# Layer 1 of a two-layer mixer: two more heads' queries beside the last recurrence, and two output jobs inside memory attention

## The reference

```python
def memory_attention(mq, mk, mv):                      # 4 heads of 128, 256 memory rows
    sc = jnp.einsum('bshd,bmhd->bhsm', mq, mk) * (MEM_HEAD_DIM ** -0.5)
    p = jax.nn.softmax(sc, axis=-1)
    return jnp.einsum('bhsm,bmhd->bshd', p, mv).reshape(B, S, MEM_W)

def lru_mixer(h, w_in, conv_w, conv_b, wa, ba, wx, bx, lam):
    xb, gate, mq = jnp.split(h @ w_in, [LRU_WIDTH, 2 * LRU_WIDTH], axis=-1)
    xc = centred_depthwise_conv(xb, conv_w, conv_b)
    y = rg_lru(xc, ..., False) + rg_lru(xc, ..., True)  # a scan forward and one backward
    return y * jax.nn.gelu(gate), mq.reshape(B, S, MEM_HEADS, MEM_HEAD_DIM)

# in first_block, for l = 1
h = rms_norm(x, mix_norm[l])
mixed, mq = lru_mixer(h, ...)
mo = memory_attention(mq, mk, mv)
x = x + jnp.concatenate([mixed, mo], axis=-1) @ w_out[l]
```

## Time and profile before

| | |
|---|---|
| median of 3 runs | 3652.66 us (3648.69 to 3657.25) |
| the profiled execution | 3656.96 us, span 3655.2 us |
| instructions | 44517 |
| mean granted PE clock over the span | 0.987 |
| PE busy over the span | 96% |
| last gate matmuls of the recurrence to the start of output job 2 | 1611.20 to 1740.99 us |
| PE busy within 1611.2 to 1741.0 | 101.44 us of 129.80 |

### The profile page before, as it was taken

The page is one execution under the profiler, slowest core; times in us unless marked ns, Lnnn a source line. Parts: engine busy times, 40 slices in busy tenths (PEclk is TensorE's granted clock), DMA queues, the critical chain, the costliest instruction groups (busy, mean ns, idle before and its releaser), DMA issues. The chain is left out here.

```text
span 3655.2 us, 44517 instructions
## 1 busy us (share of the span) xinstructions
PE 3515.4 (96%) x16494; PEld 2883.7 (79%) x16494; DVE 1723.2 (47%) x1938; ACT 984.6 (27%) x1592; POOL 1060.7 (29%) x588
## 2 busy tenths in 40 slices
PE   7989989999999999979999999999999999999999
PEld 6878878888888886757888888888688888767877
DVE  6346662533434356874254343436535434443444
ACT  3346750201010115753020101012433233202011
POOL 0111033333333330013333333333245354322350
PEclk9999999999999999989999999999999999999999
DMA  5110012111111121110211111111211111111241
GB/s 181 37 34 19 20 38 86 58 52 46 52 46 46 52 80 70 43 55 18 86 58 51 47 46 52 46 50 51 79 58 51 46 61 43 55 43 52 92 133 75
DMA packets 58439, 210.87 MB, mean 58 GB/s; under 512 B 6672, under 2 KB 11280, under 8 KB 56672
## 3 DMA queue, kind: packets, MB, share of 16 engines
q1 hardware_dynamic: 47504, 159.67, 13.4%
q10 hardware_dynamic: 10832, 49.84, 3.7%
HBM read 186.15 MB, written 22.02 MB: 57 GB/s over the span
## 5 line engine op out<-in xcount | busy, mean ns | idle before, releaser
L536 PE MATMUL G<-Hhi,whi 128*128 128x512 f32 x2528 | 1010.5, 400 | 17.0 <-issue 5.1
L536 PE MATMUL G<-Hhi,wlo 128*128 128x512 f32 x2528 | 987.3, 391 | 0.0
L536 PE MATMUL G<-Hlo,whi 128*128 128x512 f32 x2528 | 987.2, 391 | 0.0
L424 POOL CAST whi<-wraw 128x1024 fp32r<-128x1024 f32 (+1 forms) x255 | 266.2, 1044 | 2311.6 <-PE G L536 1096.7
L426 POOL TENSOR_TENSOR wlo<-wraw,whi 128x1024 fp32r<-128x1024 f32 (+1 forms) x255 | 625.3, 2452 | 20.4
L536 PEld LDWEIGHTS G<-Hhi,whi 128*128 128x128 f32 x2528 | 476.6, 189 | 127.4 <-issue 20.2
L536 PEld LDWEIGHTS G<-Hlo,whi 128*128 128x128 f32 x2528 | 476.7, 189 | 101.2 <-issue 5.7
L536 PEld LDWEIGHTS G<-Hhi,wlo 128*128 128x128 f32 x2528 | 476.1, 188 | 100.4
L536 PE MATMUL G<-Uhi,whi 128*128 128x512 f32 x1024 | 398.5, 389 | 0.0
L536 PE MATMUL G<-Uhi,wlo 128*128 128x512 f32 x1024 | 398.5, 389 | 0.0
L536 PE MATMUL G<-Ulo,whi 128*128 128x512 f32 x1024 | 398.5, 389 | 0.0
(11 more groups left out here) (341 smaller groups left out, 4759.5 us busy)
## 6 DMA issues: line engine op xcount, KB each, us to landing
wraw<-wjobs SPq DMA_DIRECT2D x292, 512.0 KB, 3.3
scratch<-X ACTq DMA_DIRECT2D x2, 4096.0 KB, 14.0
gate_tiles<-gate_st ACTq DMA_DIRECT2D x16, 512.0 KB, 2.9
T<-gate_tiles ACTq DMA_DIRECT2D x16, 512.0 KB, 3.6
X<-xT ACTq DMA_DIRECT2D x1, 4096.0 KB, 16.4
X<-xT ACTq DMA_DIRECT2D x4, 1024.0 KB, 4.9
X<-scratch ACTq DMA_DIRECT2D x4, 1024.0 KB, 4.9
X<-scratch SPq DMA_DIRECT2D x4, 1024.0 KB, 11.5
```

What stands on the lines that cost most here:

```text
L424: pool.tensor_copy(whi[:, par, 0:kt], wraw[:, par, 0:kt]).then_inc(w_hi, 1)
L536: mm = pe.matmul(G[:, par, cols], w[:, par, k, :], x[:, k, cols], start=(k == 0 and j == 0), stop=(k == kt - 1 and j == 2))
```

## The change

- The query jobs of heads 1 and 2 are made directly behind the last gate matmuls, in `lru`. Head 3's is made beside units 0 to 9.
- DVE's `memory_queries` takes a whole head at a time (1024 columns): head 0 before `behind(7, 1)`, head 1 in its middle, head 2 behind it, head 3 at unit 10. The four heads have places of their own (`MQ`), two of them where the recurrence had its inputs.
- The attention uses only `G[:, 0]` (`mem_bank`). Head 3's job and output jobs 0 and 1 use `G[:, 1]`, one behind the other: units 0 to 9, 12 to 21 and 24 to 31 with 1 or 2 parts a unit (`fill`), none in units 10, 11, 22 and 23. PE's unit 0 needs head 0, the scores of unit 2 need head 2's queries.
- Output job 0 takes the feature tiles in the order 0, 6, 1, 7, 2, 3, 4, 5. ACT casts tiles 6 and 7 at units 10 and 12, DVE subtracts at units 12 and 14. DVE adds job 0 to X at unit 22 (`add_output`), job 1 behind the attention.

```diff
@@ job_part: psum half and order of feature tiles may be given
-                k, c = q // halves, q % halves
+                i, c = q // halves, q % halves
+                k = order[i]
@@ mem_attention of PE
+                    plan = ([(0, q) for q in range(16)], [(1, q) for q in range(16)], [(2, q) for q in range(16)])
+                    fill = {}
+                    for first, counts, parts in zip((0, 12, 24), ((2, 1, 2, 1, 2, 2, 1, 2, 1, 2),) * 2 + ((2,) * 8,), plan):
+                        for v, count in enumerate(counts):
+                            fill[first + v] = [parts.pop(0) for _ in range(count)]
...
+                    if l:
+                        if v == 0:
+                            pe.wait_ge(evac[e], 3 + BASE[name][e])
+                        if v == 2:
+                            pe.wait_ge(evac[e], 3 + BASE[name][e] + 2)
+                        if v == 3 * NBLK:
+                            pe.wait_ge(evac[e], 3 + BASE[name][e] + 3)
+                        queries = MQ[h]
...
+                    if l:
+                        for m, q in fill.get(h * NBLK + u, ()):
+                            n = START[name] + 3 + m
+                            if q == 0:
+                                pe.wait_ge(evac[e], BASE[name][e] + (4 if m == 0 else 5 + m))
+                            job_part(q, n, n % 2, Hhi, Hlo, mixed_ready(1) if m else None, psum=1,
+                                     order=(0, 6, 1, 7, 2, 3, 4, 5) if m == 1 else range(KT))
@@ lru of PE
+                for h in range(1, 3):
+                    psum_waits("mq1", h, h % 2)
+                    job(START["mq1"] + h, h % 2, Hhi, Hlo, None)
@@ mem_attention of DVE
-                    if l and h + 1 < MEM_HEADS and u in (4, 7):
-                        memory_queries(h + 1, u // 7)
-                    elif l and h + 1 == MEM_HEADS and u in (4, 6):
-                        mixed_low(1, EARLY + u // 6)
+                    if l and v == 10:
+                        memory_queries(3)
+                    elif l and v in (12, 14):
+                        mixed_low(1, EARLY + v // 14)
+                    elif l and v == 22:
+                        add_output(1, 0, 1)
@@ lru of DVE
-                behind(7, 1, first_queries)
+                memory_queries(0)
+                behind(7, 1, lambda: memory_queries(1))
+                memory_queries(2)
```

More of the change, by code:

```diff
@@ L166, in build @@
         eps_col = stat[:, 30:31]
+        MQ = [T[:, 0, :], sb("MQ1", [P, S], F32, U_AT + 4 * KB)[:], sb("MQ2", [P, S], F32, U_AT + 9 * KB)[:], T[:, 1, :]]
         Q = [sb("Q0", [P, 2, S], F32, R_AT + 8 * KB), T]
@@ L356, in scored, with mem_bank, mixed_ready @@
             return G[:, par, 0:width] if u % 3 == 2 else AUX[:, u % 3, 0:width]
+        def mem_bank(l, h):
+            return 0 if l else h % 2
+        def mixed_ready(l):
+            return lambda k: (early_lo, EARLY * l + k + 1) if k < EARLY else (split_lo[l], k - EARLY + 1)
         block = ctx.enter_context(nc.Block())
@@ L523, in psum_waits, with job_part @@
                     pe.wait_ge(evac[o], (2 + BASE[name][o] if other is None else other + 2) - (par == 0))
-            def job_part(q, n, par, hi, lo, ready, kt=KT, width=S):
+            def job_part(q, n, par, hi, lo, ready, kt=KT, width=S, psum=None, order=range(KT)):
                 half = min(width, 512)
                 halves = width // half
-                k, c = q // halves, q % halves
+                i, c = q // halves, q % halves
+                k = order[i]
                 if q == 0:
@@ L535, in job_part @@
                 for j, (w, x) in enumerate(((whi, hi), (whi, lo), (wlo, hi))):
-                    mm = pe.matmul(G[:, par, cols], w[:, par, k, :], x[:, k, cols],
-                                   start=(k == 0 and j == 0), stop=(k == kt - 1 and j == 2))
+                    mm = pe.matmul(G[:, par if psum is None else psum, cols], w[:, par, k, :], x[:, k, cols],
+                                   start=(i == 0 and j == 0), stop=(i == kt - 1 and j == 2))
                 if q == kt * halves - 1:
@@ L626, in scores @@
                         pe.wait_ge(s["pr"], done + v - 2)
[L627 to L631, removed]
+                    if l:
[6 more added lines that the diff above has]
+                        queries = MQ[h]
+                    else:
+                        if b == 0:
+                            pe.wait_ge(mq_raw, h + 1)
+                        if b == 4:
+                            pe.wait_ge(evac[e], 3 + BASE[name][e] + h)
+                        queries = T[:, h % 2, :]
+                    pe.matmul(scored(mem_bank(l, h), v, 2 * P), queries[:, b * P:(b + 1) * P], MK[:, h, :], start=True, stop=True)\
                       .then_inc(s["sc"], 1)
@@ L654, in turn_result @@
                         pe.wait_ge(s["oc"], done + v)
-                    pe.transpose(G[:, v // NBLK % 2, 512:512 + P], o[:, v % 2, :], ident).then_inc(s["ot"], 1)
+                    pe.transpose(G[:, mem_bank(l, v // NBLK), 512:512 + P], o[:, v % 2, :], ident).then_inc(s["ot"], 1)
                 def beside(h, u):
-                    if h + 1 < MEM_HEADS:
+                    if l:
[5 more added lines that the diff above has]
+                                     order=(0, 6, 1, 7, 2, 3, 4, 5) if m == 1 else range(KT))
+                    elif h + 1 < MEM_HEADS:
                         for q in {1: (0, 1), 2: (2, 3), 3: (4, 5), 4: (6, 7), 5: (8, 9, 10), 6: (11, 12, 13), 7: (14, 15)}.get(u, ()):
@@ L664, in beside @@
                             pe.wait_ge(s["oc"], done + (MEM_HEADS - 1) * NBLK)
[L665 to L671, removed]
+                        for q in range(3 * u - 6, min(3 * u - 3, 16)):
+                            next_part(q, START[name] + MEM_HEADS, 0, shift, eng=e)
                 scores(0)
@@ L824, in project_out @@
             def project_out(l):
[L825 to L831, removed]
+                name, ready = f"wo_mixed{l}", mixed_ready(l)
                 pe.wait_ge(*((attns["am"]["oc"], 2 * MEM_HEADS * NBLK) if l else (attns["aw"]["oc"], KT * NBLK)))
[L833 to L837, removed]
+                if l == 0:
+                    psum_waits(name, 1, 1)
+                    for q in range(12):
+                        job_part(q, START[name] + 1, 1, Hhi, Hlo, ready)
+                    for j in range(2):
+                        for q in range(12, 16):
+                            job_part(q, START[name] + j, j, Hhi, Hlo, ready)
                 with pe.Fori(1, 4) as i:
@@ L1264, in exp @@
                     t = v % 4
-                    act.activation(pr[:, v % 2, 0:2 * P], scored(v // NBLK % 2, v, 2 * P), ACT.Exp, bias=stat[:, 4 + t:5 + t],
+                    act.activation(pr[:, v % 2, 0:2 * P], scored(mem_bank(l, v // NBLK), v, 2 * P), ACT.Exp, bias=stat[:, 4 + t:5 + t],
                                    scale=MEM_SCALE, accum_out=stat[:, 8 + t:9 + t]).then_inc(s["pr"], 1)
@@ L1276, in result @@
                     wait_apart(act, s["ot"], done + v + 1)
-                    act.copy(mo[:, h, b * P:(b + 1) * P], G[:, h % 2, 512:512 + P]).then_inc(s["oc"], 1)
+                    act.copy(mo[:, h, b * P:(b + 1) * P], G[:, mem_bank(l, h), 512:512 + P]).then_inc(s["oc"], 1)
                 if l == 0:
@@ L1291, in mem_attention @@
                         query_raw(h + 1, u // 7)
-                    elif l and h + 1 == MEM_HEADS and u in (3, 5):
+                    elif l and v in (10, 12):
                         act.wait_ge(job_done, START["wo_mixed1"])
-                        mixed_high(1, EARLY + u // 5)
+                        mixed_high(1, EARLY + v // 12)
                 result(U - 2)
@@ L1759, in start, with memory_queries @@
                 norm("nmix0", lambda k: vcol("mix_norm", k))
[L1761 to L1769, removed]
+            def memory_queries(h):
+                dve.wait_ge(job_done, START["mq1"] + h + 1)
+                dve.tensor_tensor(MQ[h], G[:, h % 2, :], rstd_1[:], ALU.mult).then_inc(evac["dve"], 1)
             def mem_attention(l):
@@ L1779, in peak @@
                     wait_apart(dve, s["sc"], done + v + 1)
-                    chain.link(dve.reduce_max(mx, scored(v // NBLK % 2, v, 2 * P), AX_X))
+                    chain.link(dve.reduce_max(mx, scored(mem_bank(l, v // NBLK), v, 2 * P), AX_X))
                     dve.tensor_scalar(negm, mx, -MEM_SCALE, None, ALU.mult).then_inc(s["mx"], 1)
@@ L1993, in mixed_low, with add_output @@
                 dve.tensor_tensor(Hlo[:, k, :], mixed[:, k, :], Hhi[:, k, :], ALU.subtract).then_inc(split_lo[l], 1)
+            def add_output(l, m, par):
+                dve.wait_ge(x_back[m // 2], l * 16 + 16)
+                dve.wait_ge(job_done, START[f"wo_mixed{l}"] + m + 1)
+                dve.tensor_tensor(X[:, m, :], G[:, par, :], X[:, m, :], ALU.add).then_inc(evac["dve"], 1)
             def project_out(l):
@@ L1997, in project_out @@
```

(11 more changed lines are left out.)

## The result

The changed kernel takes 3633.34 us (median of 7 runs, 3626.17 to 3638.30), against 3656.55 for the kernel before in the same comparison (7 runs): a ratio of 0.994 (95% interval 0.993 to 0.9949), 19 to 26 us less. The forecast was 22.2 us.

The account below looks back on a forecast made before the run. PE, busy 96% of the span, bounds the kernel, so only its idle time can be gained. Summed terms put job 2 at 1718.8 against 1740.99, 22.2 us less: 3652.66 - 22.2 = 3630.5 us, range 3622 to 3641.

Parts of the forecast that it names:

- The term of 4.1 us for the later first maximum: Attention's start: first row maximum 4.1 us later than before, first turn at 1640.2; bounds 1.25 to 6.7 us.
- The first split: POOL's split of head 3's weights meets the recurrence's last block; DVE's first L2115 (later L2151) ends 2.2 us late.
- The second: POOL's split of output job 0's weights: its cast holds the last product of DVE's recurrence for 0.8 us.
- The order forecast: End of DVE's recurrence: the sum, at 1633.0, comes before POOL's cast of output job 0's weights, at about 1633.3.
- The clock at the start: Behind PE's wait for head 2's queries (1633.8 to 1637.5), PE runs 3.6 us at the lower clock, 1.2 GHz.
- The units: Attention units on PE: 1.29 us without parts, 1.95 with one part, 2.60 with two.
- The rival in which DVE and ACT pace them: Attention units: PE no longer covers DVE and ACT, 0.5 us lost on each of 16 units; 3638.5 us, chance 0.26.
- The rival of one half of G: Attention in one half of G ties PE, DVE and ACT together; at 1 us a unit 3662.5 us, chance 0.04.
- Tiles 6 and 7: Output job 0: PE waits 2.3 us at unit 13 and 0.5 at unit 16; the clock costs another 1.7.
- The row at 1718.40: Kernel before: clock fell after a PE wait of 1.97 us; used for the 1.7 us clock cost at tile 6.
- POOL's tiles and job 1's weights: Output jobs: POOL's tiles 1 to 5 ready before their units, job 1's weights ready before unit 24.
- The tail: Attention's end: the time from the end of unit 31 to 1726.12 in the kernel before stays 2.8 us.

Follow-up runs that it names:

- the third experiment: Changed kernel with output job 0's tiles in the order 0, 1, 6, 2, 7, 3, 4, 5; 104.01 us from gates' end to job 2, ratio 0.9929.
- first: Changed kernel with output job 0's weights split on POOL only after DVE finished the recurrence; 104.59 us from gates' end to job 2, ratio 0.9922.
- second: Changed kernel with output job 0's and head 3's weights split only after DVE finished the recurrence; 106.32 us from gates' end to job 2, ratio 0.9926.
- the fourth experiment: Changed kernel with 8 of head 3's 16 parts put in PE's wait for head 2's queries; 103.24 us from gates' end to job 2, ratio 0.9923.
- the seventh: Changed kernel with output job 1 moved out of units 24 to 31, behind the attention; job 2 starts 113.3 us behind the gates' start, ratio 0.9936.
- head 1 alone: Kernel before with only head 1's query job moved behind the last gate matmuls; 128.79 us from gates' start to job 2, ratio 0.9985.
- fifth: Changed kernel with late split of output job 0's weights, its tiles reordered, and 8 head 3 parts in PE's wait; 3621.21 us, ratio 0.9903.
- sixth experiment: Changed kernel with 24 useless matmuls filling PE's wait for head 2's queries; 110.63 us from gates' start to job 2, ratio 0.9934.

## Why the prediction was right, point by point

- **The place and the size.** PE's idle time at the start of the attention is what the change uses: 22.2 us forecast, 23.4 in the stretch (135.19 to 111.75), 21.7 from the gates' end, about 22 by the ratio; the median of 3633.34 us lies within the 3626 to 3635 that the forecast gave itself. Job 2 was to start 107.6 us behind the gates' end; it starts at 108.05. Two errors of opposite sign hide in that, 2.2 us too little at the start and 1.7 too much at tile 6. The mechanism was right; that the sum came out so close is luck.
- **The start was mis-sized.** The term of 4.1 us for the later first maximum measured 6.3 (1630.22 - 1601.72 = 28.5 us behind the gates' end, before 1633.42 - 1611.20 = 22.2). The first split was right to a tenth (L2151 3.32 us). The second was to hold DVE for 0.8 us and held it for 2.7, which is 1.9 of the 2.2 us. The step that failed is the order of two instants, put at 1633.0 for the sum and 1633.3 for POOL's cast, taken from an execution whose gates ran at half clock; in the profile after they ran at full clock, PE's two jobs ended 0.6 us earlier against DVE's chain, and the cast came first. PE's wait was 5.99 us for it, where 3 to 5 had been forecast. The order forecast is seen in the third experiment, with 26.1 us against 26.3 forecast. The mechanism is shown by the first two, in which the long instructions are gone with the meeting. The rule of the Trainium skill ("SBUF — State Buffer", "Who interferes with whom"), that whichever is first holds the other for the whole instruction, agrees with both starts: the same split costs DVE's chain 0.7 or 2.7 us.
- **The clock at the start** fell as forecast (0.50 for 3.6 us), and costs 1.1 us of the path by the filled wait.
- **The units** were right: 1.90 us with one part (1.95 taken), 2.59 with two, 1.29 without, also in a row. The rival in which DVE and ACT pace them is refuted by the fourth experiment, and by the seventh but for waits of 0.67 and 0.18 us. The rival of one half of G is refuted with it.
- **Tiles 6 and 7.** The waits were 1.55 and 1.19 us, forecast 2.3 and 0.5. The clock did not fall behind the first (1.00), where the forecast took 1.7 us by a wait of 1.97; behind one of 2.38 in the fourth experiment it did. This 1.7 is what paid for the start. The row at 1718.40 was thin ground: with head 1 alone a wait of 1.97 us too, behind three shorter ones much as there (0.36, 0.54, 0.58), left the clock at full:

```profile
1711.00:1713.00 2.00, 1.97 (x11) 1.67 (x12) 0.00 (x0) 0.07 (x1) 1.92 (x2) 1.00 0.00 0
```

- **POOL's tiles and job 1's weights** were in time, as forecast.
- **The tail** is 3.1 us instead of 2.8. The trace names DVE's addition of job 1 for the last 0.84 us before job 2, though the code has job 2 wait for job 0's alone. PE waits there for ACT's last copy too; with job 1 in this place, in the seventh experiment, PE stood for 0.45 us. What the other 0.4 us are stays open.

## What to carry to other kernels

Where PE stands in front of a chain of another engine, a finished operand and a free half of PSUM are enough to put jobs there, and each is worth its length less what it makes the chain slip, as long as PE is the bound elsewhere (head 1 alone: 11.0 us of job, 3.1 of slip, 6.4 gained in all); ask next which later work their end triggers, for here it was two splits on POOL that fell into the very chain that PE waited for. A wait that has been shortened but not closed can still cost the clock behind it (5.99 and 2.38 us did here, 0.56 and 1.55 did not), so fill it first. Compare kernels over a stretch between two instructions that both have, and say in which state of the clock it began: here 5.40 or 3.70 us for the same eight matmuls, at times as much as an edit is worth.

## What the runs showed of the hardware

- Two-operand instructions of DVE in SBUF and POOL's, in the same time, wait for each other as wholes: L2151 3.32 us for 1.2, L2161 3.25 for 1.2, POOL's difference 3.20 for 2.4. DVE's products with one operand in PSUM took 1.21 us throughout. Which of them is first was decided by 0.3 us, and is worth 2 us.
- A wait of PE of 2.8 us with the same work ahead of it left the clock at full in some executions and at half in others: the same eight matmuls took 3.70 us in five of the ten profiled executions and 5.38 to 5.40 in the other five. This moves a single execution by up to 1.7 us, and the order of what follows.
- A wait of 1.55 us left the clock at 1.00, one of 2.38 was followed by 0.64 over 3 us. The length of the last wait doesn't decide alone: one of 1.97 us behind three shorter ones was followed by 0.53 in the kernel before and by 1.00 with head 1 alone, and three waits of 0.50, 0.50 and 0.83 or 0.84 us at the attention's end were followed by 0.50 to 0.59 over 3 us in the third, fifth and sixth experiment and by 1.00 in the changed kernel and in the first, second and fourth.
